# Last two expert pairs: gate and up matrices of both first, then the down matrices, the last ones in column halves

## What is computed

```python
logits = (h @ w_router + b_router)
affinity = jax.nn.softmax(logits, axis=-1)
gates, idx = lax.top_k(affinity.transpose(0, 2, 1), cap)      # cap = 64
xin = h[bidx, idx]
hid = jax.nn.silu(einsum("becd,edf->becf", xin, w_gate)) * einsum("becd,edf->becf", xin, w_up)
y = einsum("becf,efd->becd", hid, w_down) * gates[..., None]
return jnp.zeros_like(h).at[bidx, idx].add(y)
```

## Time and profile before

| | |
|---|---|
| median of three runs | 2435.66 us |
| span of the profiled execution | 2426.0 us |
| TensorE busy (matmul) | 2284.4 us, 94% |
| VectorE busy | 1058.7 us, 44% |
| ScalarE busy | 653.6 us, 27% |
| GpSimd busy | 210.6 us, 9% |
| read from HBM, mean | 590.65 MB, 244 GB/s |

### The profile page before, as it was taken

How to read it: one execution, slowest core, us unless ns; L and a number is a source line. 1 busy time by engine, 2 the same in 40 slices (tenths; PEclk the granted TensorE clock), 3 DMA queues, 4 the chain that set the end, 5 groups by cost and what they waited for, 6 DMA issues and landing times.

```text
span 2426.0 us, 25175 instructions
## 1 busy us (share of the span) xinstructions
PE 2284.4 (94%) x10601; PEld 1443.1 (59%) x10601; DVE 1058.7 (44%) x1630; ACT 653.6 (27%) x1063; POOL 210.6 (9%) x185
## 2 busy tenths in 40 slices
PE   6999999999999999999989999999989898989888
PEld 4677657888888888888768567343323333323222
DVE  5987676756654666564766535010101010101001
ACT  4233464332332423323545642101000000000000
POOL 4332020000000000000312330100000000000000
PEclk8999999999999999999999999999999999999999
DMA  8332324555542355540311207999999999999998
GB/s 333 109 104 70 139 87 156 176 189 196 197 143 72 120 191 184 180 157 22 106 36 53 96 36 310 401 430 431 430 430 430 430 431 431 431 430 430 431 431 341
DMA packets 124454, 594.41 MB, mean 245 GB/s; under 512 B 10882, under 2 KB 12432, under 8 KB 98998
## 3 DMA queue, kind: packets, MB, share of 16 engines
q1 hardware_dynamic: 120866, 583.18, 60.7%
q0 software_dynamic: 3168, 9.50, 1.2%
q10 hardware_dynamic: 308, 0.13, 0.0%
HBM read 590.65 MB, written 2.14 MB: 244 GB/s over the span
## 4 chain that ended last, share of the span: by engine, by line
PE 78%; DMA 14%; DVE 5%; ACT 2%; issue 1%; SPq 0%; POOL 0%; DVEq 0%; ACTq 0%
PE PS L1405 15%; PE PS L1133 12%; PE PS L1080 10%; PE PS L1082 10%; PE PS L1081 10%; PE PS L176 5%; PE PS L1427 4%; DMA RING<-in_w_down_dram 2%; PE PS L1442 2%; DMA RING<-in_w_gate_dram 2%; PE PS L708 1%; DMA RB_a<-in_w_up_dram 1%; DMA RB_a<-in_w_down_dram 1%; DMA HID_e<-in_w_gate_dram 1%; DMA XT<-in_w_gate_dram 1%; DMA RB_a<-in_w_gate_dram 1%
## 5 line engine op out<-in xcount | busy, mean ns | idle before, releaser
L1405 PE MATMUL PS<-RING,HID_e 128*64 128x512 f32 x576 | 205.5, 608 | 9.0 <-DMA RING<-in_w_gate_dram 5.4
L1405 PE MATMUL PS<-RB_a,HID_e 128*64 128x512 f32 x576 | 204.4, 605 | 8.0 <-DMA RB_a<-in_w_up_dram 5.4
L2928 DVE TENSOR_TENSOR TMP<-TMP,PS 128x512 f32<-128x512 f32 x32 | 19.8, 682 | 370.3 <-PE PS L1405 370.3
L696 POOL TENSOR_TENSOR WPL_e<-RING,WPH_e 128x512 fp32r<-128x512 f32 x104 | 145.8, 1413 | 300.3 <-ACT WPH_e L1516 300.3
L1405 PE MATMUL PS<-HID_e 128*64 128x512 f32 x320 | 146.0, 606 | 5.8 <-DMA HID_e<-in_w_gate_dram 2.6
L1405 PE MATMUL PS<-AT_g,HID_e 128*64 128x512 f32 x288 | 130.3, 601 | 7.3 <-DMA AT_g<-in_w_up_dram 4.7
L2069 ACT ACTIVATE HID_e<-PS,cmat 128x128 f32<-128x128 f32 x32 | 12.0, 456 | 463.7 <-PE PS L176 463.7
L1405 PE MATMUL PS<-XT,HID_e 128*64 128x512 f32 x288 | 128.6, 595 | 5.3 <-DMA XT<-in_w_gate_dram 2.7
L1133 PE MATMUL PS<-AH_e,WPH_e 128*128 128x512 f32 x320 | 128.2, 401 | 4.8 <-DVE AL_e L2284 4.0
L1133 PE MATMUL PS<-AL_e,WPH_e 128*128 128x512 f32 x320 | 126.7, 396 | 0.0
L1405 PEld LDWEIGHTS PS<-RING,HID_e 128*64 128x64 f32 x576 | 61.3, 139 | 95.5 <-issue 81.6
(11 more groups left out here) (485 smaller groups left out, 4925.4 us busy)
## 6 DMA issues: line engine op xcount, KB each, us to landing
RING<-in_w_gate_dram SPq DMA_DIRECT2D x18, 2048.0 KB, 22.1
RB_a<-in_w_gate_dram SPq DMA_DIRECT2D x18, 2048.0 KB, 22.1
RB_a<-in_w_up_dram SPq DMA_DIRECT2D x18, 2048.0 KB, 18.1
RING<-in_w_down_dram SPq DMA_DIRECT2D x18, 2048.0 KB, 22.1
RB_a<-in_w_down_dram SPq DMA_DIRECT2D x18, 2048.0 KB, 22.1
RING<-in_w_up_dram SPq DMA_DIRECT2D x17, 2048.0 KB, 17.0
RING<-in_mlp_w_dram SPq DMA_DIRECT2D x32, 1024.0 KB, 5.3
RB_a<-in_mlp_w_dram SPq DMA_DIRECT2D x32, 1024.0 KB, 5.2
```

The lines of the kernel that those rows point to most:

```text
L696: pool.tensor_tensor(WPL[:, n % 4, :], ring.view(*parts[b][1:], k // 4)[:, k % 4, :], WPH[:, n % 4, :].bitcast(F32), ALU.subtract).then_in ...
L1405: last = pe.matmul(b[64 * d:64 * d + 64, :], xv_[:, k, 64 * d:64 * d + 64], wv, start=k == 0, stop=k == 7)
L2928: dve.tensor_tensor(q, q, banks.of("up", n, fg), ALU.mult).then_inc(*V_moe.up("act", n, fg))
```

## The change

- **Order.** Pairs 0 to 5 stay. For pairs 6 and 7 the loads are: gate and up of 6, gate and up of 7, down of 6, down of 7. TensorE follows: `pe_up` 6, the turn of 6, `pe_up` 7, down 6, down 7.
- **Turn of pair 7.** It lies in down 6, two steps behind row 1 and two behind row 3, with banks 2 and 3. `hidT` has a second buffer for pair 7 (the place of `Pm` and `Pg`, which are dead by then), so ScalarE's copy no longer waits for the down product of pair 6.
- **Scatter of pair 6.** No longer between the gate matmuls of pair 7; its four blocks lie behind rows 2, 3, 4 and 5 of down 7.
- **The last 8 rows of pair 7's down matrices** come by column halves: first columns 0 to 511 of rows 8 to 15, in four pieces of 1 MB, then columns 512 to 1023 in two pieces of 1 MB and four of 512 KB. A partition's share of a row is then 2 KB. The pieces use the same four slots of 2 MB, and there are 10 loads in place of 16.
- **TensorE's end.** Rows 8 to 15 for the first half; rows 8 to 11 for the second half; four scatter matmuls of the first half; rows 12 to 15 for the second half; four scatter matmuls of the second half. VectorE weights and adds by halves, and the stores go by halves.

The number of matmuls, transposes, copies and adds is that of before. The diff, without the declaration of ten instead of sixteen semaphores and with few lines around each edit:

```diff
@@ -413,7 +413,7 @@
         xins = [HID3[:, 5120 + 1024 * i:5120 + 1024 * (i + 1)].rearrange("p (k n) -> p k n", k=8) for i in range(2)]
-        hidT = HID3[:, 7168:9216].rearrange("p (f n) -> p f n", n=128)
+        hidTs = [HID3[:, o:o + 2048].rearrange("p (f n) -> p f n", n=128) for o in (7168, 10240)]
         hid_tmp = Turns([TMP[:, i, :] for i in range(4)])
@@ -488,8 +488,10 @@
 
+        last_pieces = (((0, 4), (4, 8)), ((0, 4), (4, 6), (6, 8)))
+
         def sp_experts(sp, w):
-            for n in range(8):
+            def gate_and_up(n):
                 for m in range(2):
@@ -506,17 +508,30 @@
                                 big.many, big.i = 7, 0
-                for kq in range(4 if n < 7 else 2):
+
+            def down(n, kqs=range(4)):
+                for kq in kqs:
                     for d in range(2):
...
                                  (T_moe, "dn", n, kq))
-            for kq in (2, 3):
-                views = [big.claim(w, ("dn", 7, kq, d), (4, 1024), (T_moe, "dn", 7, kq)) for d in range(2)]
-                for k in range(4 * kq - 8, 4 * kq - 4):
+
+            for n in range(6):
+                gate_and_up(n)
+                down(n)
+            gate_and_up(6)
+            gate_and_up(7)
+            down(6)
+            down(7, range(2))
+            i = 0
+            for hf in range(2):
+                views = [big.claim(w, ("last", hf, d), (8, 512)) for d in range(2)]
+                for k0, k1 in last_pieces[hf]:
                     for d in range(2):
                         rows8 = A["w_down_2"][0, 14 + d].rearrange("(h p k) n -> h p k n", h=2, k=8)
-                        sp.dma_start(views[d][:, k % 4, :], rows8[1, :, k, :]).then_inc(*D[f"last{2 * k + d}"].up())
+                        sp.dma_start(views[d][:, k0:k1, :], rows8[1, :, k0:k1, 512 * hf:512 * hf + 512]).then_inc(
+                            *D[f"last{i}"].up())
+                        i += 1
 
@@ -581,8 +596,8 @@
             sp_experts(sp, w)
-            for i in range(4):
-                for hf in range(2):
+            for hf in range(2):
+                for i in range(4):
                     w.wait_ge(*V_moe.at("sc", 7, i, hf))
@@ -1378,7 +1393,7 @@
 
-            if n and k < 4:
+            if 0 < n < 7 and k < 4:
                 pe_scatter(pe, w, n - 1, k)
@@ -1386,7 +1401,7 @@
         def pe_moe_turn(pe, w, n, t):
-            b = banks.seat(w, t, ("hid", n, t), (S_moe, "hid", n, t))
+            b = banks.seat(w, 2 + t % 2 if n == 7 else t, ("hid", n, t), (S_moe, "hid", n, t))
             w.wait_ge(*V_moe.at("act", n, t | 1))
@@ -1413,34 +1428,71 @@
 
+        def pe_down_block(pe, w, n, k, hf, b, wv, landed):
+            w.wait_ge(*S_moe.at("hid", n, k // 4))
+            for d in range(2):
+                w.wait_ge(*landed(d))
+                last = pe.matmul(b[64 * d:64 * d + 64, :], hidTs[n // 7][:, k, 64 * d:64 * d + 64], wv(d), start=k == 0,
+                                 stop=k == 15)
+            return last
+
+        def pe_down_rows(pe, w, n, k, bs):
+            for hf, b in enumerate(bs):
+                last = pe_down_block(pe, w, n, k, hf, b,
+                                     lambda d: big.view("dn", n, k // 4, d)[:, k % 4, 512 * hf:512 * (hf + 1)],
+                                     lambda d: big.landed("dn", n, k // 4, d))
+            if k % 4 == 3:
+                last.then_inc(*T_moe.up("dn", n, k // 4))
+
         def pe_down(pe, w, n):
-            for t in range(4):
-                pe_moe_turn(pe, w, n, t)
-            bs = [banks.seat(w, 4 + hf, ("down", n, hf), (V_moe, "y", n, hf)) for hf in range(2)]
+            if n < 6:
+                for t in range(4):
+                    pe_moe_turn(pe, w, n, t)
+            bs = [banks.seat(w, (0 if n == 6 else 4) + hf, ("down", n, hf), (V_moe, "y", n, hf)) for hf in range(2)]
             for k in range(16):
-                w.wait_ge(*S_moe.at("hid", n, k // 4))
-                for hf, b in enumerate(bs):
-                    for d in range(2):
-                        w.wait_ge(*(D[f"last{2 * (k - 8) + d}"].all() if n == 7 and k > 7 else
-                                    big.landed("dn", n, k // 4, d)))
-                        wv = big.view("dn", n, k // 4, d)[:, k % 4, 512 * hf:512 * (hf + 1)]
-                        last = pe.matmul(b[64 * d:64 * d + 64, :], hidT[:, k, 64 * d:64 * d + 64], wv,
-                                         start=k == 0, stop=k == 15)
-                if k % 4 == 3:
-                    last.then_inc(*T_moe.up("dn", n, k // 4))
+                pe_down_rows(pe, w, n, k, bs)
                 if n == 0 and k in (3, 7):
...
                     pe_gate_turn(pe, w, 1)
+                elif n == 6 and k in (1, 3):
+                    pe_moe_turn(pe, w, 7, k - 1)
+                    pe_moe_turn(pe, w, 7, k)
+
+        def pe_last_down(pe, w):
+            bs = [banks.seat(w, 4 + hf, ("down", 7, hf), (V_moe, "y", 7, hf)) for hf in range(2)]
+            for k in range(8):
+                pe_down_rows(pe, w, 7, k, bs)
+                if 2 <= k < 6:
+                    for hf in range(2):
+                        pe_scatter_half(pe, w, 6, k - 2, hf, (2, 3, 6, 7)[(2 * k + hf) % 4])
+
+            def half(hf, first, pieces):
+                for i, (k0, k1) in enumerate(pieces):
+                    for k in range(k0, k1):
+                        last = pe_down_block(pe, w, 7, 8 + k, hf, bs[hf], lambda d: big.view("last", hf, d)[:, k, :],
+                                             lambda d: D[f"last{first + 2 * i + d}"].all())
+                return last
+
+            half(0, 0, last_pieces[0]).then_inc(*T_moe.up("down", 0))
+            half(1, 4, last_pieces[1][:1])
+            for i in range(4):
+                pe_scatter_half(pe, w, 7, i, 0, (2, 3, 6, 7)[i])
+            half(1, 6, last_pieces[1][1:]).then_inc(*T_moe.up("down", 1))
+            for i in range(4):
+                pe_scatter_half(pe, w, 7, i, 1, (0, 1, 2, 3)[i])
 
...
             for hf in range(2):
-                b = banks.seat(w, 4 + (2 * i + 2 + hf) % 4, ("sc", n, i, hf), (V_moe, "sc", n, i, hf))
-                w.wait_ge(*V_moe.at("y", n, hf))
-                pe.matmul(b, PTm[n % 2][:, i * 128:(i + 1) * 128], yB[:, hf * 512:(hf + 1) * 512], start=True,
-                          stop=True).then_inc(*T_moe.up("sc", n, i, hf))
+                pe_scatter_half(pe, w, n, i, hf, 4 + (2 * i + 2 + hf) % 4)
+
+        def pe_scatter_half(pe, w, n, i, hf, seat):
+            b = banks.seat(w, seat, ("sc", n, i, hf), (V_moe, "sc", n, i, hf))
+            w.wait_ge(*V_moe.at("y", n, hf))
+            pe.matmul(b, PTm[n % 2][:, i * 128:(i + 1) * 128], yB[:, hf * 512:(hf + 1) * 512], start=True,
+                      stop=True).then_inc(*T_moe.up("sc", n, i, hf))
 
@@ -1473,11 +1525,15 @@
             pe_gather(pe, w, 0, 0)
-            for n in range(8):
+            for n in range(6):
                 pe_up(pe, w, n)
                 pe_down(pe, w, n)
-            for i in range(4):
-                pe_scatter(pe, w, 7, i)
+            pe_up(pe, w, 6)
+            for t in range(4):
+                pe_moe_turn(pe, w, 6, t)
+            pe_up(pe, w, 7)
+            pe_down(pe, w, 6)
+            pe_last_down(pe, w)
 
@@ -2078,9 +2134,11 @@
             w.wait_ge(*T_moe.at("hid", n, fg))
-            if n:
+            if n == 7:
+                w.wait_ge(*T_moe.at("pt", 7))
+            elif n:
                 w.wait_ge(*T_moe.at("dn", n - 1, 3))
-            act.activation(hidT[:, 4 * fg:4 * fg + 4, :], banks.of("hid", n, fg).rearrange("p (k n) -> p k n", n=128),
+            act.activation(hidTs[n // 7][:, 4 * fg:4 * fg + 4, :], banks.of("hid", n, fg).rearrange("p (k n) -> p k n", n=128),
                            ACT.Copy, bias=0.0, scale=1.0).then_inc(*S_moe.up("hid", n, fg))
@@ -2865,10 +2923,24 @@
                 for hf in range(2):
-                    o = acc[:, i, hf * 512:(hf + 1) * 512]
-                    w.wait_ge(*T_moe.at("sc", n, i, hf))
-                    w.wait_ge(*(V_moe.at("sc", n - 1, i, hf) if n else G_moe.at("acc", i, hf)))
-                    dve.tensor_tensor(o, banks.of("sc", n, i, hf), o, ALU.add).then_inc(*V_moe.up("sc", n, i, hf))
+                    dve_scatter_half(dve, w, n, i, hf)
+
+        def dve_scatter_half(dve, w, n, i, hf):
+            o = acc[:, i, hf * 512:(hf + 1) * 512]
+            w.wait_ge(*T_moe.at("sc", n, i, hf))
+            w.wait_ge(*(V_moe.at("sc", n - 1, i, hf) if n else G_moe.at("acc", i, hf)))
+            dve.tensor_tensor(o, banks.of("sc", n, i, hf), o, ALU.add).then_inc(*V_moe.up("sc", n, i, hf))
+
+        def dve_weighted(dve, w, n, hf):
+            dve.tensor_tensor(yB[:, hf * 512:(hf + 1) * 512], banks.of("down", n, hf),
+                              g2b[:, hf * 512:(hf + 1) * 512], ALU.mult).then_inc(*V_moe.up("y", n, hf))
+
+        def dve_act(dve, w, n):
+            for fg in range(4):
```

(28 more changed lines are left out.)

## The result

The changed kernel takes 2439.85 us in the median of 20 executions (2431.5 to 2444.62), the kernel before, beside it on the same chip, 2433.36 us (2424.73 to 2438.5). The ratio is 1.0023, with a 95% interval of 1.0014 to 1.0033: slower by 5.6 us (3.4 to 8.0); the two medians themselves differ by 6.49 us. That is just over the 0.2% named in the prediction. The profiled execution of the changed kernel has a span of 2440.3 us and took 2442.55 us.

What follows compares the result with a forecast made beforehand. Weight transfer sets the pace up to the last experts; in the tail transfer and TensorE are level. Terms of -1.13, +8.15, -2.8, +3.6 and -3.44 us gave +4.4 us, 2440.1 us; range 2436.5 to 2444.5.

Steps and rivals of the forecast that it cites:

- What stays: Expert stage loads: landings by position stay, down 7's first quarter 2383.40, second 2393.14; the queue never runs dry.
- Step 1: Turn of pair 7 moved into down 6: hidden there, down 7 begins at its quarter's landing, -1.13 us.
- Step 2: Scatter of pair 6 inside down 7: nothing hides it, four pairs at 2.04 us each, +8.15 us.
- Step 3: Waits of the old tail: TensorE has work from 2383.40 to the end, so they go, -2.8 us.
- Step 4: Column halves at the end: four scatter matmuls come earlier, +3.6 us; four adds leave the end, -3.44 us.
- Step 5: Landing of the 2 KB-row halves: last piece between 2413.5 and 2417.8, early enough for TensorE; nothing added.
- Step 6: TensorE's granted clock behind the wait before down 7: a fall costs 1.7 us; the sum assumed none.
- The 9.66 us around the span: Whole execution: profiled span plus 9.66 us was taken to be the median time, 2435.66 us before the change.
- The clock rival: Start of down 7: the clock falls and nothing hides it, +4.4 + 1.7 us, 2441.8 us; chance 0.28.
- Transfer late: Last halves: 2 KB rows reach only, say, 270 GB/s, down product ends at 2426.0; 2443.3 us, chance 0.12.
- transfer sets the end: End of down 7: the last landing, not TensorE, decides; -3.1 us, 2432.6 us, chance 0.11.

Runs made afterwards that it cites:

- e6: Column halves in the order of before, plus pair 7's last up quarter taken bank by bank so down 7 starts earlier; tail 53.42 us, one execution 2425.98 us.
- e1: Changed kernel without three of the four blocks of pair 6's scatter; tail 53.30 us against the changed kernel's 58.63, ratio to before 0.9991.
- e4: Changed kernel with the first block of pair 6's scatter moved into the wait ahead of down 7; tail 55.11 us, ratio to before 1.0015.
- e3: Changed kernel with the new order alone, last 8 rows in whole-row pieces as before; tail 56.85 us against before's 52.34, ratio to before 1.0016.
- e2: Kernel before, in its old order, with only the column halves added; tail 53.40 us against 52.34, ratio to before 1.0005.
- e5: Changed kernel with eight matmuls that compute nothing in the wait before down 7; tail 57.15 us against 58.63, ratio to before 1.0005.

## Why the prediction was right, and where not

The absolute number, 2440.1 us against 2439.85, is better than its parts. The forecast difference was +4.4 us, the tail's is +6.29, and the timed ratio gives 5.6 (3.4 to 8.0). The kernel before had 2433.36 us in this comparison instead of the 2435.66 on which the sum was put, which hid 2.3 us: that the time came out so close is luck. The mechanism was right but for one step of the sum, the clock, which was decided the wrong way.

- **What stays.** Right. Down 7's first quarter by the forecast's position is 2383.40 + 8.01 = 2391.41; TensorE starts on it at 2391.45. Its second quarter landed at 2401.1, against 2401.15. The queue did not run dry.
- **Step 1, the turn.** Right in where it goes. TensorE starts down 7 on the landing, and that the four turn groups lie in down 6 shows nowhere behind it. What the step did not say is that the 1.13 us gained are gained ahead of a landing. e6 shows that the same gain in the old order comes to nothing, because the next quarter holds TensorE. In the new order scatter 6 fills that wait.
- **Step 2, scatter 6.** Right: 2.04 us a pair, measured 2.05. Its sign is shown from both sides, by e1 (three pairs less, -5.33) and by e4 (one pair hidden, 2.05 of its -3.52).
- **Step 3, the 2.8 us of waits.** Right in the new order, for in e3 the sum without the halves holds to 0.35 us (56.85 against 56.5). But the step read them as waits that go by themselves. They are 1.7 us for the second quarter of down 7 (due at 2391.45, started at 2393.14), of which the row showed 0.67, and some 1.1 us for the last pieces. They are filled only because scatter 6 stands there. In e2, where it does not, I counted them as gained again and was 3.7 us off. The reader should see that a wait for a landing is no reserve: work put ahead of it is hidden, but nothing that follows starts earlier.
- **Step 4, the halves.** Right to 0.2 us. Four scatter matmuls inside took 3.63 us, and with the row behind them (3.61 us for 16 records, 3.46 in a pure stream) 3.78 instead of 3.6. First to last add are 2434.65 to 2437.23, 2.58 us as forecast.
- **Step 5, the landings.** Right, near the early bound. The ten pieces, 8.39 MB, landed between 2403.6 and 2421.7, the last 20.6 us behind the second quarter, some 408 GB/s; in before the same bytes took from 2393.1 to 2413.0, 422 GB/s. TensorE needed the last piece at about 2430.9 and had 9 us to spare. The Trainium skill, DMA: Bandwidth & Descriptors, section Bandwidth, gives 341 GB/s for one transfer of 1 MB; here pieces of 0.5 and 1 MB, queued behind each other, move 408.
- **Step 6, the clock.** Here the forecast failed, and its own sign of being wrong, a dip of the clock behind the start of down 7, came true. The sum went by the nearer wait, 2373.66, which has no fall; but 2391.45 is another wait, and being the neighbour of one without a fall says nothing of it. It fell in three profiles of three, from about 2391.2 to 2394.6, and cost 1.53 us by e3's first rows, 1.48 us by e5. The clock rival had it right, priced at 1.7 from a whole quarter: 52.34 + 4.4 + 1.7 = 58.44, measured 58.63 to 58.66. I had given it 0.28 from one wait of each kind. Counted over the whole expert stage of before, 18 waits of TensorE for weights are longer than 2 us (1707.88 to 2373.66); behind 9 of them the clock is 0.72 to 0.76 over 6 us, behind the other 9 it is 1.00. The chance was thus about one half by the trace that I had, and the fall belonged in the sum as a coin toss of 1.7 us. In before each such fall is followed by another wait for weights, which takes up the loss; in after the last one is not.
- **The 9.66 us around the span.** Wrong. Each execution's time is its span and 2.2 us (2442.55 and 2440.3 in after). The profiled execution of before was therefore one of about 2428.2 us, and 7.4 of the 9.66 us are the difference between two executions. It did no harm, because only a difference of spans was added to the median.
- **The rivals.** Transfer late and transfer sets the end are both excluded by the landings: TensorE has no wait between 2391.45 and 2432.72, and the down product ends 11 us after the last landing.

Put together: 4.4 us as forecast, 1.5 us of clock, 0.2 us in step 4, and 0.2 us by which the first three rows are longer than a pure stream even without a fall (5.36 us in e3 against 3 x 1.73) make 6.3.

What stays open: whether the clock falls at this wait by a habit of after or by chance. It fell in after's three profiles and in e1's, and not in e3's, whose instructions up to there are the same but for the loads' pieces. The waits ahead differ, though. In all three of after's profiles, and in e4's and e5's, falls stand behind the waits 68 and 49 us ahead of down 7 (in after 2323.39 and 2342.80, clock 0.76 and 0.72); in e3 only the later of the two has one. So e4 and e5 came to the last wait with after's history and differ from it in the filled wait, which speaks for the filling; e3 came with another, and its full clock may be chance. Single profiles of e3, e4 and e5 don't show how often it stays up there, so e4's 1.5 us and e5's 1.48 are differences between one profile each.

## What to carry to other kernels

Work that sat in a transfer's waits was free there and cost its full time (2.05 us a pair) once it was moved into a stretch that the engine bounds; before you reorder loads, list what the waits of the old order hide and where each piece will stand. A wait for a landing is not time to be won by work saved ahead of it, and its row may show less than the wait if a parallel column group ran ahead. Where an engine-bound stretch begins behind a wait, count how many such waits of the trace are followed by a fall of the clock and price it in by that share; and measure such a change from a landmark just ahead of the edit.

## What the hardware showed that I had not expected

- Two executions of one kernel differ by up to 14 us (before: 2424.73 to 2438.5), in stages that no edit touches. It goes with TensorE's mean granted clock over the span: in before's runs 0.985 to 0.987 at 2425.0 to 2425.6 us, 0.978 to 0.981 at 2436 to 2438.7; in after's 0.983 to 0.985 at 2431.5 to 2433.9, 0.977 to 0.980 at 2440 to 2444.6. The 8 us between the two profiled executions build up in steps: 3.75 us by 353 us, 5.8 by 1198, 7.95 by 1247, and then hardly more. Whether falls of the clock cause the spread was not tried.
- Rows of 2 KB cost almost nothing while the queue is full: 408 GB/s against 422, 0.7 us over 8.39 MB, in the one profile of after against the one of before.
- With eight matmuls of 128 columns that compute nothing in a 2.7 us wait the clock behind it stayed at 2.4 GHz, in the one profile taken of that (e5).
